# Small fp32 products of one Trainium2 core as 64x64 tiles of TensorE, in a hybrid decoder block

## The reference, cut to what matters

```python
# recurrence, for each chunk of 64 tokens and each head (q_, k_, v_, g_ of the chunk)
b = jnp.cumsum(g_, axis=2)
o_inter = jnp.einsum('bhck,bhkv->bhcv', q_ * jnp.exp(b), state)
diff = b[:, :, :, None, :] - b[:, :, None, :, :]
decay = jnp.where(causal, jnp.exp(jnp.where(causal, diff, 0.0)), 0.0)
scores = jnp.einsum('bhik,bhjk,bhijk->bhij', q_, k_, decay)
o = o_inter + jnp.einsum('bhij,bhjv->bhiv', scores, v_)
state = (jnp.exp(b_last[:, :, 0, :])[..., None] * state
         + jnp.einsum('bhck,bhcv->bhkv', k_ * jnp.exp(b_last - b), v_))
# pooling: one 64x64 matrix for each of the four groups
y = jnp.einsum('bsgc,gcd->bsgd', pooled, w_grp)
```

## Time and profile before

| | |
|---|---|
| median of 3 timed runs | 2347.45 us |
| the profiled execution, its own time | 2343.45 us |
| its span, first to last instruction | 2341.7 us |
| TensorE (PE) busy | 2275.6 us, 97% |
| VectorE (DVE) busy | 1256.7 us, 54% |
| ScalarE (ACT) busy | 772.3 us, 33% |
| GpSimd (POOL) busy | 229.4 us, 10% |
| mean granted clock of TensorE | 0.992 of full speed |
| L704 (levels 1 to 6), matmul records | 384, mean 282 ns |
| L804 (A by values), matmul records | 128, mean 273 ns |
| L739, L813 (64x64), matmul records | 256 each, mean 222 and 221 ns |
| L793 (pool weights), matmul records | 16, mean 592 ns |

### The profile page before, as it was taken

The page is one execution under the profiler, slowest core; times in us unless marked ns, Lnnn a source line. Parts: engine busy times, 40 slices in busy tenths (PEclk is TensorE's granted clock), DMA queues, the critical chain, the costliest instruction groups (busy, mean ns, idle before and its releaser), DMA issues.

```text
span 2341.7 us, 33056 instructions
## 1 busy us (share of the span) xinstructions
PE 2275.6 (97%) x11291; PEld 1837.2 (78%) x11307; DVE 1256.7 (54%) x2145; ACT 772.3 (33%) x1500; POOL 229.4 (10%) x151
## 2 busy tenths in 40 slices
PE   6999899999999999999999999999999999999997
PEld 4776688788788778888888778888888877888886
DVE  3648484675766555152556745334355665515345
ACT  3535433343344432121134532113024344212212
POOL 2322244444300000000000000000000000000000
PEclk9999999999999999999999999999999999999999
DMA  9963688878563446555564254655546334655555
GB/s 362 353 223 137 223 293 301 283 272 300 212 256 112 144 145 249 187 191 197 188 221 150 73 198 167 233 194 196 196 163 235 109 144 156 226 193 197 194 187 193
DMA packets 115396, 483.14 MB, mean 206 GB/s; under 512 B 7999, under 2 KB 38985, under 8 KB 69705
## 3 DMA queue, kind: packets, MB, share of 16 engines
q1 hardware_dynamic: 115273, 481.53, 56.8%
HBM read 378.74 MB, written 102.76 MB: 206 GB/s over the span
## 4 chain that ended last, share of the span: by engine, by line
PE 90%; DVE 5%; issue 1%; DMA 1%; SPq 1%; ACT 1%; DVEq 0%; ACTq 0%
PE ps L606 18%; PE ps L608 18%; PE ps L607 18%; PE ps L631 8%; PE ps L633 8%; PE ps L632 8%; PE ps L704 2%; PE ps L728 1%; PE ps L839 1%; PE ps L827 1%; PE ps L670 1%; PE ps L548 1%; PE ps L804 1%; SPq L291 1%; DMA AWT<-in_w_ada_dram 1%
## 5 line engine op out<-in xcount | busy, mean ns | idle before, releaser
L606 PE MATMUL ps<-hTh,wt 128*128 128x512 f32 x1920 | 758.4, 395 | 12.9 <-DVE hTl L1470 8.7
L608 PE MATMUL ps<-hTh,wt 128*128 128x512 f32 x1920 | 748.4, 390 | 0.0
L607 PE MATMUL ps<-hTl,wt 128*128 128x512 f32 x1920 | 748.1, 390 | 0.0
L606 PEld LDWEIGHTS ps<-hTh,wt 128*128 128x128 f32 x1920 | 360.9, 188 | 105.5 <-issue 26.8
L608 PEld LDWEIGHTS ps<-hTh,wt 128*128 128x128 f32 x1920 | 360.7, 188 | 76.3
L607 PEld LDWEIGHTS ps<-hTl,wt 128*128 128x128 f32 x1920 | 361.2, 188 | 71.5
L1704 DVE TENSOR_SCALAR cv<-ub,CW 128x512 f32<-128x512 f32 x176 | 98.2, 558 | 472.5 <-ACT ub L1315 458.0
L1315 ACT ACTIVATE ub<-ps 128x512 f32<-128x512 f32 x176 | 105.3, 598 | 689.7 <-PE ps L608 689.7
L631 PE MATMUL ps<-wt,pTh 128*128 128x512 f32 x704 | 275.1, 391 | 1.9 <-ACT T L1082 1.9
L633 PE MATMUL ps<-wt,pTh 128*128 128x512 f32 x704 | 274.0, 389 | 0.0
L632 PE MATMUL ps<-wt,pTl 128*128 128x512 f32 x704 | 273.9, 389 | 0.0
(11 more groups left out here) (243 smaller groups left out, 2350.3 us busy)
## 6 DMA issues: line engine op xcount, KB each, us to landing
wt<-split_w SPq DMA_DIRECT2D x268, 1024.0 KB, 4.8
split_w<-wt SPq DMA_DIRECT2D x88, 1024.0 KB, 7.0
raw<-in_w_up_dram SPq DMA_DIRECT2D x22, 1024.0 KB, 9.6
XT<-in_w_ada_dram SPq DMA_DIRECT2D x10, 1024.0 KB, 11.5
XN<-in_x_dram SPq DMA_DIRECT2D x5, 2048.0 KB, 9.2
raw<-in_w_in_dram SPq DMA_DIRECT2D x8, 1024.0 KB, 13.7
XR<-in_x_dram SPq DMA_DIRECT2D x4, 2048.0 KB, 10.3
raw<-in_w_down_dram SPq DMA_DIRECT2D x8, 1024.0 KB, 9.2
```

Source lines behind the costliest of these rows:

```text
L606: mm(ps[:, bank, :], w, hTh[:, k, :], start=(k == 0), stop=False)
L607: mm(ps[:, bank, :], w, hTl[:, k, :], start=False, stop=False)
L608: ins = mm(ps[:, bank, :], wl[:, slot, k, :], hTh[:, k, :], start=False, stop=(k == KD - 1))
```

## The change

- The levels: every product of 128x128 becomes four of 64x64, one for each chunk c of the tile and each head of the pair (par). Rows by head, output partitions by chunk, PSUM bank by head. Only pairs of the same chunk are computed. ZR loses its zero half (32 moving columns for each product), L1570 goes, and `level_mul` makes ZR in one instruction of 128 partitions. Level 0 has one moving column of `ones` instead of `hsel`.
- The wait for the operands (`z_ready`, `qk_ready`) now comes last ahead of a level and is a fence.
- A has 64 columns for a tile and head (partitions by chunk) instead of 128: `level_take` writes half as much. Level 0's `ident` is replaced by `eye`, two 64x64 identities one above the other, and its instruction by two. `hgmask` is folded to 32 columns.
- The products of A with the values become 32 of 64x64, rows and output partitions both by chunk. The products with the states wait for the last two of them by a new semaphore, `intra_mm`.
- The pool weights: four products of 64x64 with 512 columns, rows and output partitions both by group.
- Memory: the modulation's weights, which used A's and ZR's places before those exist, keep places of the same size under names of their own.

```diff
-ACT_STEPS, DVE_STEPS, UP_STEPS = 28, 105, 16
+ACT_STEPS, DVE_STEPS, UP_STEPS = 28, 98, 16
...
+        eye = sb("eye", [P, CH])
-        hsel = sb("hsel", [P, 2])
...
-        A = mb("A", [P, TT, HH, P])
+        wide_a = ExitStack()
+        AWA = sb("AWA", [P, 4, 512], fp32, wide_a)
+        wide_a.close()
+        A = mb("A", [P, TT, HH, CH])
+        mb("A_rest", [P, 1024])
...
-        ZR = sb("ZR", [P, 2, 2 * TT, P], fp32, early)
+        wide = ExitStack()
+        AWZ = sb("AWZ", [P, 4, 512], fp32, wide)
+        wide.close()
+        ZR = sb("ZR", [P, 2, 2 * TT, P // 2], fp32, early)
...
+            step(pool.tensor_copy(hgmask[64:128, :, 0:32], hgmask[64:128, :, 32:64]))
+            for q in range(2):
+                step(pool.tensor_copy(eye[64 * q:64 * q + 64, :], ident[64 * q:64 * q + 64, 64 * q:64 * q + 64]))
...
-            for par in range(2):
-                for q in range(2):
-                    step(pool.memset(hsel[64 * par:64 * par + 64, q:q + 1], float(par == q)))
...
-                    if o:
-                        pe.wait_ge(s["z_ready"], b * 6 + o)
-                    else:
-                        pe.wait_ge(s["qk_ready"], b + 1)
                     if o >= 2:
                         pe.wait_ge(s["level_taken"], b * 13 + (2 * o - 3))
                     if tok and o % 2:
                         pe.wait_ge(s["tok_taken"], b * 7 + tok)
+                    if o:
+                        fenced(s["z_ready"], b * 6 + o)
+                    else:
+                        fenced(s["qk_ready"], b + 1)
                     for t in range(TT):
                         for j in range(2):
-                            if o:
-                                col = (2 * (t % 2) + j) * P
-                                ins = mm(ps[:, 4 + 2 * (o % 2) + t // 2, col:col + P],
-                                         ZB[:, (o - 1) % 2, j * BT + t * P:j * BT + t * P + P],
-                                         ZR[:, (o - 1) % 2, j * TT + t, :], start=True, stop=True)
-                            else:
-                                col = 4 * t + 2 * j
-                                ins = mm(ps[:, 4, col:col + 2], R[:, j, t * P:t * P + P], hsel[:], start=True, stop=True)
+                            for c in range(2):
+                                for par in range(2):
+                                    r = slice(64 * par, 64 * par + 64)
+                                    to = slice(64 * c, 64 * c + 64)
+                                    tok0 = t * P + 64 * c
+                                    if o:
+                                        col = (2 * t + j) * 32
+                                        ins = mm(ps[to, 4 + 2 * (o % 2) + par, col:col + 32],
+                                                 ZB[r, (o - 1) % 2, j * BT + tok0:j * BT + tok0 + 64],
+                                                 ZR[r, (o - 1) % 2, j * TT + t, 32 * c:32 * c + 32], start=True, stop=True)
+                                    else:
+                                        col = 2 * t + j
+                                        ins = mm(ps[to, 4 + par, col:col + 1], R[r, j, tok0:tok0 + 64], ones[r, 0:1],
+                                                 start=True, stop=True)
                     ins.then_inc(s["level_mm"], 1)
...
                     fenced(s["pool_ready"], b + 1)
                     for a in range(2):
-                        ins = mm(ps[:, 6 + a, :], PW[:, a, :], R[:, a, :], start=True, stop=True)
+                        for q in range(2):
+                            r = slice(64 * q, 64 * q + 64)
+                            ins = mm(ps[r, 6 + a, :], PW[r, a, r], R[r, a, :], start=True, stop=True)
                     ins.then_inc(s["pool_mm"], 1)
...
                     for t in range(TT):
                         for h in range(HH):
                             bank, cols = place(t, h)
-                            mm(ps[:, bank, cols], A[:, t, h, :], VH[:, t, h * 64:h * 64 + 64],
-                               start=(t == 0 and h < 2), stop=False)
-                    fenced(s["qe_ready"], b + 1)
+                            for c in range(2):
+                                r = slice(64 * c, 64 * c + 64)
+                                ins = mm(ps[r, bank, cols], A[r, t, h, :], VH[r, t, h * 64:h * 64 + 64],
+                                         start=(t == 0 and h < 2), stop=False)
+                                if t == TT - 1 and h == HH - 1:
+                                    ins.then_inc(s["intra_mm"], 1)
+                    pe.wait_ge(s["qe_ready"], b + 1)
+                    fenced(s["intra_mm"], b * 2 + 2)
                     for t in range(TT):
...
-                    for par in range(2):
-                        r = slice(64 * par, 64 * par + 64)
-                        step(tt(ZR[r, l % 2, :, r].rearrange("p a (n w) -> p a n w", w=w),
-                                z[r, :, w:2 * w].rearrange("p (a n) w -> p a n w", a=2 * TT),
-                                q[r, :, w:2 * w].rearrange("p (a n) w -> p a n w", a=2 * TT), ALU.mult))
+                    step(tt(ZR[:, l % 2, :, :].rearrange("p a (n w) -> p (a n) w", w=w),
+                            z[:, :, w:2 * w], q[:, :, w:2 * w], ALU.mult))
                     tt(z[:, :, 0:w], z[:, :, 0:w], k[:, :, 0:w], ALU.mult).then_inc(s["z_ready"], 1)
...
                         dve.wait_ge(s["level_mm"], b * 7 + 1)
-                        tt(A[:].rearrange("p t h n -> p (t h) n"), ident[:].unsqueeze(1).to_broadcast([P, 16, P]),
-                           ps[:, 4, 0:16].unsqueeze(2).to_broadcast([P, 16, P]), ALU.mult).then_inc(s["level_taken"], 1)
+                        heads_a = A[:].rearrange("p t h n -> p (t h) n").rearrange("p (a par) n -> p par a n", par=2)
+                        for g in range(2):
+                            ins = tt(heads_a[:, g], eye[:].unsqueeze(1).to_broadcast([P, 8, CH]),
+                                     ps[:, 4 + g, 0:8].unsqueeze(2).to_broadcast([P, 8, CH]), ALU.mult)
+                            if g:
+                                ins.then_inc(s["level_taken"], 1)
+                            else:
+                                step(ins)
                         return
                     w = LEVELS[o - 1]
                     fenced(s["level_taken"], b * 13 + (2 * o - 1))
                     fenced(s["level_mm"], b * 7 + o + 1)
                     for g in range(2):
-                        src = ps[:, 4 + 2 * (o % 2) + g, :].rearrange("p (a n w) -> p a n w", a=8, w=w)
-                        dst = A[:, 2 * g:2 * g + 2, :, :].rearrange("p t h (n w) -> p (t h) n w", w=2 * w)[:, :, :, w:2 * w]
-                        m = hgmask[:, o - 1, :].rearrange("p (n w) -> p n w", w=w)\
-                            .unsqueeze(1).to_broadcast([P, 8, 64 // w, w])
+                        src = ps[:, 4 + 2 * (o % 2) + g, 0:256].rearrange("p (a n w) -> p a n w", a=8, w=w)
+                        dst = A[:].rearrange("p t h n -> p (t h) n").rearrange("p (a par) (n w) -> p par a n w", par=2, w=2 * w)\
+                            [:, g, :, :, w:2 * w]
+                        m = hgmask[:, o - 1, 0:32].rearrange("p (n w) -> p n w", w=w)\
+                            .unsqueeze(1).to_broadcast([P, 8, 32 // w, w])
                         V.copy_predicated(dst, m.bitcast(i32), src).then_inc(s["level_taken"], 1)
...
-                for par in range(2):
-
-                    step(ts(ZR[64 * par:64 * par + 64, :, :, 64 * (1 - par):64 * (1 - par) + 64]
-                            .rearrange("p a b n -> p (a b) n"),
-                            ident[64 * par:64 * par + 64, 64 * (1 - par):64 * (1 - par) + 64].unsqueeze(1)
-                            .to_broadcast([64, 4 * TT, 64]), 0.0, None, ALU.mult))
```

8 lines of the change are left out of this document (4 added, 4 removed).

## The result

| | before | after |
|---|---|---|
| median of 4 timed runs, us | 2347.55 (2346.28 to 2348.02) | 2324.73 (2323.56 to 2327.33) |
| the profiled execution, us | 2343.45 | 2325.23 |
| its span, us | 2341.7 | 2323.5 |
| mean granted clock of TensorE | 0.992 | 0.989 |

The change makes the kernel faster: the ratio is 0.9909, 95% interval [0.9895, 0.9922]. Between the medians lie 22.8 us, between the two profiled executions 18.2 us. The profiled execution of before was 4.1 us quicker than its own median, that of after 0.5 us slower than its own. All that follows explains the 18.2 us; the other 4.6 are the scatter of single executions (a second set of runs gave 2346.22 and 2326.24, 20.0 us apart).

The account below looks back on a forecast made before the run. TensorE, busy 97% of the span, was taken to bound the kernel. Three blocks at -4.8 us and the first at -2.7 made -17.1, from the median 2347.45 to 2330.3 us, range 2321 to 2340.

Parts of the forecast that it names:

- The price of a run of 64x64 tiles: 64 small records standing alone between large products hold TensorE 1.33 us, of which entering and leaving are 0.33.
- Joined runs: A run of 64 records joined to another of the same tile size costs 1.0 us more; a second fence 0.07.
- Three lone levels and the two pairs: Per block: levels 2, 3, 4 together -1.38 us; diagonal with level 1 -1.17; level 5 with chunk states -0.72.
- Level 6: Last level, between two other tile shapes: 1.86 us becomes 1.33, -0.53 a block.
- The recurrence: Intra-chunk products 1.95 us in place of 3.61, plus a new wait of 0.35: 4.81 becomes 3.5, -1.31 a block.
- The pool weights: Four 64x64 products instead of two wide ones save nothing; entering and leaving come on top: +0.3 us a block.
- The first block: Savings ahead of the modulation's transfers only lengthen TensorE's wait: -2.7 us; up to 2.1 come back if loads come earlier.
- the swings of up to 1.7 each way: TensorE's clock at places like the head of the FFN may shift, each worth up to 1.7 us either way.
- two bounds for the fences: Seven fences ahead of the levels: at worst 1.7 us a block; in the range, up to 1.0 a block more.
- (A): Diagonal quarters sharing a PSUM bank in the intra-chunk and pool products don't run side by side: 2344.7 us, no change; 8%.
- (C): The floor of 25 ns from start to start holds for the new small product shapes: 2346 us; 2%.
- (B): Two runs in a row outpace TensorE's instruction supply, second run at 0.06 us a record: +15 us, 2362; 5%.

Follow-up runs that it names:

- run 6: The changed kernel with the levels streaming 64 columns (the 32 of ZR read twice) in place of 32: 2322.50 us (one run).
- run 8: The kernel before, its 128x128 products untouched, with a fence for the operands ahead of each of the seven levels: 2345.84 us, ratio 1.0006.
- pool_wide: The changed kernel with the pool weights put back as two products of 128x128: 2323.31 us, ratio 0.9909.
- pool_wide_2: The changed kernel with the pool weights as two 128x128 products, run again as control: 2321.03 us, ratio 0.9890.
- four_quarters: The changed kernel with pool weights 128x128 again and odd heads' intra-chunk products moved to the two idle quarters: 2319.72 us, ratio 0.9883.
- run 4: The changed kernel with the products of A by the values made for all of one chunk half, then the other: 2331.11 us (one run).
- runs 11: The changed kernel with the chunk states' 32 products made twice, so 192 records stand in a row with level 5: 2338.64 us (one run).
- 12: The kernel with the chunk states made twice, plus 112 semaphore increments ahead of level 4 in the later blocks: 2392.96 us (one run).
- run 3: The changed kernel with each level's products made for all of one row half, then the other: 2346.97 us (one run).
- runs 5: The changed kernel with the 32 products of each of the seven levels made twice: 2379.02 us, ratio 1.0139.

## Why the prediction was right

The forecast was 2330.3 us, in the range 2321 to 2340, and 2324.73 was measured. The mechanism and the sign of every term came out. Between the profiled executions the saving was 18.2 us against the 17.1 forecast; the 22.8 between the medians are in part luck (see the sum).

*The price of a run of 64x64 tiles.* The step read 1.33 us for a lone run off L739; it is 1.27 (0.94 for 64 records and 0.33 for entering and leaving, of which the 0.09 ahead is now seen by itself). Levels stream half the columns or one, and run 6 shows that this matters by 0.02. Joined runs add 0.97 and 1.01, close to the 1.0 taken, so the 0.07 for a second fence was too much: fences are free (run 8). Three lone levels and the two pairs were undersized by 0.46 us a block together.

*Level 6* was the worst-sized term, -0.53 against -0.87. Ahead of it 0.10 us went with the wait for VectorE's states. The prediction had said so ("this wait goes too", unless the narrower copies cost as much as the wide ones) and put nothing into the sum for it. The copies did get shorter (1.32 for 2.48), and 1.09 us of slack came of it. The other 0.24 come from the way out: next to the attention's shapes the run pays less than the 0.33 taken from runs between large products. Some of the attention's records are missing in both traces, so I don't divide it further.

*The recurrence* came out at 3.56 for 3.5. From the last A product's start to the first of the states' it is 0.40 us, where the step had 0.35 and one pace of 15 ns. *The pool weights* cost 0.33 more, as the sum had it.

*The first block* was forecast at 2.7 us, and the profiled executions differ by 0.9 to 1.0 up to the second block's diagonal. Counted from its own diagonal the block gave 3.0, and in the second profiled execution of the change (after_again) 0.6: the term lies inside what two executions of one kernel give, and luck decides on which side. The step had this: what is saved ahead of the modulation's transfers "only lengthens that wait". By the large products with the same number in both traces 2.9 us are saved ahead of XT (the diagonal with level 1 gives 1.4, levels 2 and 3 0.7 each), where the step had 2.1. 2.0 of them are waited away, 0.8 come through, and after_again agrees to 0.1. That XT came 1.3 us later than in before is the 2.1 us lost at 44 to 50 us, less this 0.8; in after_again XT came 0.8 us earlier. What the step left out is the clock behind the longer wait: the ten large products behind level 4 take 5.06 us in place of 4.17, 6.24 in after_again, and between 4.8 and 6.5 in the other profiled kernels whose levels are 64x64. The other swings come where nothing changed: 2.1 us at 44 to 50 us, and 1.7 at 632 us (20 large products in 8.44 us for 6.70; 6.7 to 6.9 in pool_wide, pool_wide_2 and four_quarters).

*The sum.* Three blocks at -5.4 and the first at -1.0 make -17.2. The other -1.1 lie between the pool weights and the next block's diagonal. At the two passages from one later block to the next TensorE had waited (0.68 us ahead of L606 at 1209.17) and hardly does now: -0.7 and -0.9, in the other profiled kernels with the change's levels too. The prediction has no term for it, and why this wait went is not shown. At the head of the FFN the clock took 1.5 and 0.4 us in the second and third block and gave back 1.4 in the fourth, the swings of up to 1.7 each way that the prediction allowed for. Of the 5.6 us by which the median came out under the forecast, 4.6 are that the profiled execution of before was quick for its kernel, and of after an ordinary one: luck of the executions. The prediction also gives two bounds for the fences, 1.7 us a block and 1.0; the sum uses neither, and run 8 shows none of it.

*The rivals.* (A) is refuted by the change's own trace and by run 4. The Trainium skill ("TensorEngine Tiling (Array Packing)", Gotcha 1) has different row tiles barred from one PSUM bank at the same time; in L820 and L807 two of them write disjoint partitions of one bank, and the pace is that of two working at once (2.08 us against 3.76 in turn). (C) is refuted too: 64 records of L715 start within 0.92 us, 15 ns apart, under the floor of about 25 ns that the Trainium skill gives ("TensorE: Matmul & The Clock Gate", "Wait — 56ns, not 53.3ns?"). (B) was nearer than its 5%. TensorE does outrun its supply of instructions, but as a pause of 0.7 to 5.2 us where a packet lands late, and not as a slower pace in each record as the rival had it. No group of the change was hit: all of its groups cost the same in the three later blocks, to 0.01 us, and no such pause stands in its first. By runs 11 and 12 what spared them was the place of their code: luck, for no reason in the prediction excluded it.

## What to carry to other kernels

Small fp32 products whose weights are narrow gain from 64x64 tiles if consecutive ones go to different quarters, the row halves in turns; the order of the loops decides it (run 3 lost all). Price such a run by the distance between the large products around it, and add about 0.33 us for entering and leaving; where the moving side is long, as in the pool weights, leave the wide tile alone. When small records come by the hundred, look for "issue" pauses at the same record in every iteration: they move with the code ahead of them.

## What the runs showed of the hardware

- For fp32 tiles of 64x64, a quarter takes a record each 0.056 to 0.062 us whether it streams 1, 32 or 64 columns, and four quarters in rotation give one each 15 ns. Products that change row half only once per 32 products gain nothing over 128x128 tiles (1.99 us a level against 1.80).
- Two diagonal quarters that write disjoint partitions of one PSUM bank work at once.
- A wait with an increment behind it ahead of a group costs nothing that ten runs can see (ratio 1.0006, [0.9996, 1.0016]); 112 increments in a row idle TensorE for 13.3 us.
- Instructions come in packets of 16 KB, each some 0.9 to 2.3 us on its queue in these runs. In runs 5, 11 and 12 TensorE idled 0.7 to 5.2 us at twelve places among small products, each time went on 1.1 to 1.5 us after a packet had landed, and ran slower for a time behind some of them (granted clock 0.70 over 1841.4 to 1843.8 in run 5).
- TensorE's clock behind a wait differs from one execution to the next of the same kernel: over 44 to 50 us the change was granted 0.57 in one and 1.00 in another, 2.1 us apart.
